# A hybrid decoder block on 8 cores: when the W_o casts in DRAM, the late x tiles and the GLU scaling are issued

## The reference, cut to what matters

```python
xn   = rms_norm(x, g_pre_mix)
[q|k|v|u] = xn @ w_in                          # 1024 + 256 + 256 + 1024 columns
attn = sliding_window_attention(rotary(q), rotary(k), v, sinks)   # window 128, 16 heads on 4
y    = s5_ssm(u, ...)                          # 64 groups of 16 channels, 64 complex states each
z    = gelu(y)
ssm  = z * sigmoid(z @ w_glu + b_glu)
mix  = concat[rms_norm(attn), rms_norm(ssm)] @ w_o
h    = x + rms_norm(mix)
out  = h + rms_norm(silu(hn @ w_gate) * (hn @ w_up) @ w_down)     # hn = rms_norm(h), 5632 columns
```

## Time and profile before

| | us |
|---|---|
| median of 3 executions | 2664.11 |
| lowest of them | 2650.02 |
| the profiled execution | 2658.24 |
| its span on the slowest core (core 4) | 2656.7 |
| spans of the 8 cores in it | 2602.2 to 2656.7 |

### The profile page before, as it was taken

How to read it: one execution, slowest core, us unless ns; L and a number is a source line. 1 busy time by engine, 2 the same in 40 slices (tenths; PEclk the granted TensorE clock), 3 DMA queues, 4 the chain that set the end, 5 groups by cost and what they waited for, 6 DMA issues and landing times.

```text
span 2656.7 us, 33801 instructions; the slowest of 8 cores (2602.2 to 2656.7 us)
## 1 busy us (share of the span) xinstructions
PE 2487.2 (94%) x12896; PEld 1215.4 (46%) x12896; DVE 1559.8 (59%) x2436; ACT 826.7 (31%) x1632; POOL 573.7 (22%) x650
## 2 busy tenths in 40 slices
PE   4999778888898889999999999999999999999998
PEld 2546546753444334444444444444444444444443
DVE  6865763677767777787778510006787877710003
ACT  5534433356555432222222100003322232200002
POOL 0234644654433301010101111000101010111112
PEclk8888778998899999999999999999999999999999
DMA  9644769666576877767676976649999967675557
GB/s 261 150 82 76 91 106 141 97 151 167 147 192 184 198 160 115 110 84 92 83 92 83 174 128 102 98 67 162 174 172 180 152 80 95 85 122 76 76 107 234
DMA packets 479773, 341.82 MB, mean 129 GB/s; under 512 B 182016, under 2 KB 442496, under 8 KB 470656
## 3 DMA queue, kind: packets, MB, share of 16 engines
q0 software_dynamic: 260944, 173.10, 48.6%
q1 hardware_dynamic: 218672, 166.57, 23.8%
HBM read 406.65 MB, written 63.96 MB: 177 GB/s over the span
## 4 chain that ended last, share of the span: by engine, by line
PE 78%; DMA 9%; DVE 6%; issue 2%; ACT 2%; POOL 2%; SPq 1%; POOLq 0%; DVEq 0%
PE ps L433 78%; DMA ws.6_48<-w_in 2%; SPq L433 1%; DMA qT.3_45<-qr.85_127 1%; DMA uring.90_132<-uscr 1%; DVE ast.27_69 L433 1%; DVE ast.26_68 L433 1%; DMA raw.149_191<-w_up 1%; DMA kT.4_46<-qr.84_126 1%; DMA PT.126_168<-Pb.123_165 1%; DMA PT.127_169<-Pb.124_166 1%; DVE attn.128_170 L433 0%; DVE xr.138_180 L433 0%; DVE Rb.103_145 L433 0%; DVE M1.2_44 L433 0%
## 5 line engine op out<-in xcount | busy, mean ns | idle before, releaser
L433 ACT ACTIVATE ps<-ps 128x512 f32<-128x512 f32 x96 | 55.8, 581 | 352.9 <-DVE ev.176_218 L433 138.5
L433 DVE TENSOR_TENSOR hf.235_277<-ps,gpo.190_232 128x512 f32<-128x512 f32 x16 | 11.1, 692 | 243.4 <-ACT junk.145_187 L433 233.6
L433 PE MATMUL ps<-hnT.144_186,wsm.152_194 128*128 128x512 bf16 x528 | 121.1, 379 | 0.0
L433 PE MATMUL ps<-hnT.144_186,wsm.153_195 128*128 128x512 bf16 x528 | 121.1, 379 | 0.0
L433 PE MATMUL ps<-hnT.144_186,wsm.154_196 128*128 128x512 bf16 x528 | 121.1, 379 | 0.0
L433 PE MATMUL ps<-hnT.144_186,wsm.151_193 128*128 128x512 bf16 x528 | 121.0, 379 | 0.0
L433 DVE TENSOR_TENSOR wsm.154_196<-raw.150_192 128x1024 bf16<-128x1024 bf16 x110 | 68.7, 686 | 63.2 <-DMA raw.150_192<-w_gate 60.8
L433 DVE TENSOR_TENSOR wsm.151_193<-raw.147_189 128x1024 bf16<-128x1024 bf16 x110 | 69.1, 690 | 54.8 <-DMA raw.147_189<-w_gate 54.8
L433 ACT ACTIVATE junk.145_187<-ps 128x512 bf16<-128x512 f32 x16 | 9.6, 597 | 253.4 <-PE ps L433 253.4
L433 DVE TENSOR_TENSOR wsm.153_195<-raw.149_191 128x1024 bf16<-128x1024 bf16 x110 | 69.9, 685 | 21.7 <-DMA raw.149_191<-w_up 21.7
L433 POOL DMA_DIRECT2D raw.150_192<-w_gate x22 | 25.2, 1145 | 258.7 <-PE ps L433 179.7
(11 more groups left out here) (1373 smaller groups left out, 6242.3 us busy)
## 6 DMA issues: line engine op xcount, KB each, us to landing
raw.147_189<-w_gate POOLq DMA_DIRECT2D x22, 1024.0 KB, 11.7
raw.148_190<-w_up POOLq DMA_DIRECT2D x22, 1024.0 KB, 10.3
raw.150_192<-w_gate POOLq DMA_DIRECT2D x22, 1024.0 KB, 11.5
raw.149_191<-w_up POOLq DMA_DIRECT2D x22, 1024.0 KB, 13.0
woscr<-w_o POOLq DMA_DIRECT2D x16, 512.0 KB, 9.7
xr.138_180<-x SPq DMA_DIRECT2D x8, 1024.0 KB, 6.3
xr.139_181<-x SPq DMA_DIRECT2D x8, 1024.0 KB, 6.6
hscr<-xr.138_180 SPq DMA_DIRECT2D x8, 1024.0 KB, 4.5
```

What stands on the lines that cost most here:

```text
L433: inst = getattr(eng, m)(*a, **kw)
```

## The change

Of the casts, nine may now start after u products 14, 16, 18 and so on to 30 (counted from 0, by ScalarE's copies of them), and seven after pairs 8, 10, 12, 14, 16, 18 and 20; none after a rope copy. The four w_glu casts follow pairs 9, 13, 17 and 21 in place of 16, 19, 22 and 25. Tile 4 of x still follows the first half of the u weights, tiles 5 and later follow the second. The GLU scaling of blocks 0 to 2 has priority 480 in place of 405, so gates of the next block that are ready go first. The planner's length of a POOL DMA issue is 0.6 for one that writes DRAM and 1.15 for others, in place of 1.1.

```diff
-        op.dur = (1.2 if tr else 0.57) if q == "sync" else 1.1
+        op.dur = (1.2 if tr else 0.57) if q == "sync" else (0.6 if "DRam" in type(out.tensor).__name__ else 1.15)
...
-                P.dma(b[:, :], x[tt * 128:(tt + 1) * 128, :], rk=[("wu", 0)] if tt > 3 else ())
+                P.dma(b[:, :], x[tt * 128:(tt + 1) * 128, :], rk=[("wu", 0 if tt == 4 else 1)] if tt > 3 else ())
...
             for tb in range(4):
+                P.prio = GPRIO
...
-                if tb == 3:
-                    P.prio = 590.0
+                P.prio = 590.0 if tb == 3 else 480.0
...
+        P.prio = 20.0
+        for n, i in enumerate((14, 16, 18, 20, 22, 24, 26, 28, 30)):
+            cast_wo(n, usteps[i])
...
-            if q in (14, 17, 20, 23, 26, 29):
-                cast_wo((14, 17, 20, 23, 26, 29).index(q), last)
-            if q in (16, 19, 22, 25):
-                i = (16, 19, 22, 25).index(q)
+            if q in (8, 10, 12, 14, 16, 18, 20):
+                cast_wo(9 + (8, 10, 12, 14, 16, 18, 20).index(q), last)
+            if q in (9, 13, 17, 21):
+                i = (9, 13, 17, 21).index(q)
...
-        for n, i in enumerate((10, 18, 22, 26, 30, 34, 38, 42, 46, 50)):
-            P.prio = 62.0
-            cast_wo(6 + n, psteps[i])
```

More of the change, by code:

```diff
@@ L778, in bank3 @@
             return bk
+        usteps = []
         def proj_u(h):
@@ L789, in proj_u @@
                                      rhs=xnT[:, c, tb * 512:(tb + 1) * 512], start=(c == 0), stop=(c == 15))
-                    A.activation(out=ust[:, 3 - blk, :, tb * 64:(tb + 1) * 64],
-                                 in_=ps[:, bk, :].rearrange("p (c j) -> p j c", j=8), func=AF.Copy)
+                    usteps.append(A.activation(out=ust[:, 3 - blk, :, tb * 64:(tb + 1) * 64],
+                                               in_=ps[:, bk, :].rearrange("p (c j) -> p j c", j=8), func=AF.Copy))
                 if n >= 12 if h == 0 else n % 4 == 3:
@@ L815, in load_h @@
             return w
-        psteps = []
         def rope(bk, tt, n):
             rr, rA, rB = rbuf[n % 2]
-            psteps.append(A.activation(out=rr[:, :], in_=ps[:, bk, 0:256], func=AF.Copy))
+            A.activation(out=rr[:, :], in_=ps[:, bk, 0:256], func=AF.Copy)
             V.tensor_tensor(out=rA[:, :], in0=rr[:, :], in1=cap(cosT, tt * 32, [[512, 128], [0, 8], [1, 32]]), op=ALU.mult)
```

## The result

The changed kernel took 2623.59 us in the median of five executions, the kernel before 2664.11; the ratio is 0.9871, with a 95% interval of 0.983 to 0.9912. Medians are over all executions; the ratios leave out those in which the cores of one die ran some per cent longer at a lower clock. The forecast of 2633 us was 10 us above the time measured, which lies inside the range and within 2% of before. The sum was nearly right, but its terms were not: at full clock the casts cost several times the 7 us allowed at their new place, and gave back more than the 28 at the old one. Some 8 us more than forecast were gained between the first gate product and the first feed-forward product, a stretch of which only the GLU scaling had a term.

What follows compares the result with a forecast made beforehand. Late transfers beside W_o casts were taken to cost TensorE 37 us from 350 to 510 us. From 2658: 28 gained by casts, 7 lost early, 0 for x tiles, 4 gained by GLU, giving 2633 us; range 2608 to 2660.

Steps and rivals of the forecast that it cites:

- The sum: Whole kernel: 2658 - 28 + 7 + 0 - 4 = 2633 us; all ends good 2603, all bad 2674.
- The casts out of the q pieces: From 350 to 510 us: without eleven casts, transfers land sooner; 28 us gained, between 14 and 37.
- The casts into u products and early pairs: From 100 to 270 us: eleven added casts raise DMA share to 69%; 7 us lost, between nothing and 21.
- the cover: From 70 to 240 us: TensorE, busy 169.33 of 170 us, has other work while casts delay transfers.
- Middle pairs and w_glu casts: Middle pairs: five casts replace five, so no change within 5 us; moving four half-size w_glu casts costs nothing.
- x tiles: At the start: second u-weight half lands 3 to 6 us earlier, later x tiles lose it; 0, 4 either way.
- GLU scaling: GLU blocks: scalings yield to the next block's gates, so rbc is free earlier; 4 us gained, between 0 and 9.
- The planner's lengths: POOL DMA issues in the planner: the new lengths only set the order; no gain or loss given.
- Rival A: Early pairs: casts make ring loads late, 42.5 us lost against 32 gained; 2669 us, chance 0.14.

Runs made afterwards that it cites:

- its second run: The kernel before, unchanged, run again on another chip for a profile at full clock: median 2643.91 us, ratio 1.0015.
- the second run of the changed kernel: The changed kernel, unmodified, run again on the chip of the follow-up runs, against the kernel before: median 2625.01 us, ratio 0.9927.

## Why the prediction was right, point by point

*The casts out of the q pieces* (28 us, up to 37). The mechanism was right. The transposes land in 3.2 us, the casts are gone, and from the first q product to the last (385.6 to 522 us on core 2) TensorE is busy 126.30 of 136.40 us, 93%, where over 90% had been said. The stretch from zraw to the last q product fell by 36 us at full clock (173.4 to 137.3) and the one from the end of pair 27 to zraw by 4 (42.0 to 37.8): 40 us, above the upper end. Some 8 of them belong to the last four pairs, whose end (`A1T.68`) comes 18.5 us later (339.2 to 357.7) where that of pair 27 comes 26.7 later. Scaling the loss by 0.76, since the share would only fall to 55%, was too careful: at 0.59 to 0.61 nothing of it was left. (The waits named in the prediction are seven, not eight, to add up to 27.2 us.)

*The casts into u products and early pairs* (7 us lost, at most 21). This is the step that failed. At full clock the last use of A1T.67 came 26.7 us later (311.1 to 337.8), above the upper end. 22.2 of them are there at the end of pair 15 (225.0 to 247.2), which the early casts alone precede. Two things were wrong in the term. The share of 69% was a mean over 170 us; the casts follow u products, and eight of them fall into 80 us, where the engines were full. And the cover was read in a run in which TensorE had the clock of 0.82: u products lasted until 223 us on that core instead of 201 to 210, which gave the transfers time. At that clock the term was near: on the two cores of the first run that had 0.82 throughout, A1T.67 was last used at 342 us, against 330 to 334 on the six such cores of the kernel before, some 10 us. It named ring loads as what would be late; the u stores ahead of them and the A1T transposes on SP's queue were late too, and VectorE stood at the transposes. (The weights that it calls those of the first q pieces are the second load of `wh.8`, the second column's; the count of eleven casts ahead of it holds.) A transfer's room is not only that of the load that TensorE waits for: here it is a chain of three, u store, ring load and operator transpose, and VectorE's own buffers hang on it. The rule that DMAs of all engines interleave on the same 16 (the Trainium skill, DMA: Bandwidth & Descriptors, "Issuing engines are not separate DMA queues") agrees with the trace here: SP's A1T transposes land after 6.4 to 19.3 us beside POOL's casts, 2.7 to 3.6 without.

*Middle pairs and w_glu casts* (0, 5 either way). No run took them alone, but the traces divide the loss: 22.2 us at the end of pair 15, 26.7 at that of pair 27, so 4.5 between, inside the 5. This may still be late work of the early casts.

*x tiles* (0). Right: with the lengths and x tiles alone the last u product stands within 0.4 us of before. In the first pair of runs the second half of `ws.6` lands after 39.9 us on the slowest core, not after 48.00, 8 us sooner where 3 to 6 had been estimated; but a load of `ws.7` rose from 12.4 to 18.1 us, and the first u product starts at 39 us in both. On core 4 x tiles 5 to 8 land 0.5 to 1.6 us later. What one transfer gains the next ones lose, as the term had it.

*GLU scaling* (4 us, up to 9). Right in size and place: 5.8 us on the kernel before, 4.1 on the changed one. The wait of TensorE for rbc (4.8 us in the earlier trace rows) is not among those of the changed kernel. The tile rbc there:

```profile
its engine sat idle before it (us, times) until:
  ACT rbc.14_56 L433: 1.6, 1
who waited for it (us, times):
  DVE M1.2_44 L433: 1.6, 1
  ACT L430: 1.4, 1
```

The whole stretch fell by 11.5 us, since the moved casts alone shorten it by 8 and the lengths alone by 9, and that was in no term. What does it was not settled. In the kernel before, the cores that end their q pieces late also take longer afterwards (in its second run core 0 ends at 538 us and takes 383, core 4 at 513 us and takes 369), so the late end itself may be the cause. But its first run shows no such order (core 7 ends at 512 us and takes 383, core 5 at 540 us and takes 372), and no run separates it.

*The planner's lengths* were put down as setting only the order. So they do, but the order was worth 16 us by itself, and nothing beside the moved casts. Had the casts stayed, that would have been an error of the sum.

*The sum.* 26.7 - 40.3 - 11.5 and 0.3 elsewhere make 24.8 us less at the first feed-forward product (534.7 + 377.0 against 521.4 + 365.5), at full clock, where the second run of the changed kernel took 24 us less in the median. The forecast was 25 less, by 7 - 28 - 4. That it came out right was luck: the early casts cost 20 us more than their term, the q pieces gave 12 more and the stretch after the gates 8 more, and these errors cancel. At the clock of the prediction's own profile they are other ones. Between the slowest cores of the first two profiles (core 4 before, core 2 changed) the pairs end 8.4 us later (334.1 to 342.5), from there to the first gate product it takes 34.1 less (222.2 to 188.1), and from there to the feed-forward network 12.9 less (380.9 to 368.0): 39 us, where those executions differ by 35 and 25 had been forecast. There the 7 was near, and the forecast was 10 us high by its gains. Rival A, with 0.14, had the mechanism, a loss there by late transfers, but both of its sizes wrong: a loss of 42.5 us, as a bound, where 26.7 were measured, against a gain of 32, where 52 were (40.3 and 11.5).

## What to carry to other kernels

A transfer that is moved off one stretch has to be placed in the next by what it meets there, not by a mean share. With eight of its casts in 80 us, beside the u stores, the changed kernel's pairs end 27 us later; with eight casts one in 21 us, after the u products, they end no later. The rate alone doesn't settle it: in the kernel with the casts spread, at one in 22 us, they end 16 us later than before, largely because two casts left together beside a transpose that was needed next. So look for a DMA share near 1.0 in windows as short as the transfers themselves (0.75 over 80 us was 1.03 over 16), and count what hangs on each transfer in it. And when a profile shows a clock below full in the stretch that is to be the cover, take the cover from a core or a run with full clock: the same casts cost the pairs some 10 us at 0.82 and 27 at full clock.

## What the runs showed of the hardware

The granted clock from 70 to 240 us was not a property of the kernel. In the first run of the kernel before six cores had 0.80 to 0.82 there and two (cores 6 and 7, on a die with cores 4 and 5) 0.99 to 1.00; in the second run, on another chip, all had 0.97 to 1.00. In the first run of the changed kernel cores 2 and 3 alone had 0.82, and in the second none (0.93 to 0.96, with gaps in TensorE's work). Yet with all eight cores in the feed-forward network, from 980 to 1800 us, the clock is 1.00 on every core of these four runs. What sets it in the head was not found.

At a DMA share of 1.0 from 130 to 210 us the casts took 15.2 us from issue to landing in the median on core 4 of the changed kernel and 21.3 on core 7 of the kernel with four A1 buffers, against 8.1 on core 4 of the kernel with eight casts, where they stand among pairs (210 to 270 us). On that core 7 small and large transfers landed alike, eight 64 KB ring loads after 19.0 us and four 512 KB u stores after 22.4; in the kernel before, on the same core and stretch, after 3.1 and 7.7. So the small ones lost the larger factor there, six against three. It does not hit all of them: three loads of the other ring landed after 8.0 us there, and on core 4 of the changed kernel eight after 2.8.
